# A decoder layer on one core: block rows spread by a VectorE transpose, decay rows loaded from DRAM, two groups of transposes moved to other slots

## The reference, cut to what matters

```
h = rms_norm(x)
all projections = h @ w_in                      # 2048 x 12304
branch A (8 heads x 128): causal softmax attention with ALiBi, times silu(gate)
branch B (8 heads x 128): short conv + silu on q, k, v; gated delta rule, per-head norm, times silu(gate)
x = x + (sigmoid(gA) * (A @ w_a) + sigmoid(gB) * (B @ w_b)) @ w_out ; rms_norm
```

## Time and profile before

| | |
|---|---|
| median of 3 runs | 800.74 us (800.04 to 801.30) |
| the profiled execution | 799.87 us |
| its span in the trace | 798.2 us |
| PE busy | 787.4 us (99%) |
| PE weight loads | 650.2 us (81%) |
| DVE busy | 519.4 us (65%) |
| ACT busy | 408.6 us (51%) |
| POOL busy | 103.3 us (13%) |
| loaded and stored | 142 MB, 178 GB/s |

### The profile page before, as it was taken

One profiled execution on the slowest core, in us unless ns is written; L12 is line 12 of the kernel. 1 busy time (PEld: TensorE's weight loads), 2 busy tenths in 40 slices (PEclk: granted clock), 3 DMA queues, 4 the chain that ended last, 5 costly groups with the idle time before them and its releaser, 6 DMA issues.

```text
span 798.2 us, 12578 instructions
## 1 busy us (share of the span) xinstructions
PE 787.4 (99%) x3712; PEld 650.2 (81%) x3712; DVE 519.4 (65%) x1030; ACT 408.6 (51%) x625; POOL 103.3 (13%) x174
## 2 busy tenths in 40 slices
PE   8999999999999999999999999999999999999996
PEld 7878888888888888888888888888888888888884
DVE  5687558646855785487558647855784556765563
ACT  5755545545554645455455455554545654444450
POOL 7020201110101012010201110101012000001120
PEclk9999999999999999999999999999999999999998
DMA  9946655575656555746655565656555666578652
GB/s 248 261 126 182 173 160 172 153 201 157 184 158 164 167 168 160 196 144 183 183 159 163 162 189 144 184 158 188 154 178 160 186 198 191 173 252 273 202 165 106
DMA packets 179225, 142.16 MB, mean 178 GB/s; under 512 B 10897, under 2 KB 144257, under 8 KB 179073
## 3 DMA queue, kind: packets, MB, share of 16 engines
q1 hardware_dynamic: 179056, 141.59, 61.2%
q10 hardware_dynamic: 144, 0.26, 0.1%
HBM read 139.72 MB, written 2.10 MB: 178 GB/s over the span
## 4 chain that ended last, share of the span: by engine, by line
PE 95%; DVE 2%; issue 1%; DMA 1%; ACT 0%; SPq 0%; POOLq 0%; POOL 0%; DVEq 0%; ACTq 0%
PE pj L542 28%; PE pj L540 28%; PE pj L541 28%; PE dn_ps L592 1%; DVE w_lo L1082 1%; PE pj L828 1%; PE pj L827 1%; PE pj L826 1%; PE dn_ps L621 1%; PE dn_ps L616 1%; DMA w_raw<-in_w_in_dram 1%; PE dn_ps L579 1%; PE dn_ps L605 0%; DVE conv L1202 0%; PE mo_ps L651 0%
## 5 line engine op out<-in xcount | busy, mean ns | idle before, releaser
L1082 DVE TENSOR_TENSOR w_lo<-w_raw,w_hi 128x1024 fp32r<-128x1024 f32 x251 | 309.5, 1236 | 163.6 <-ACT w_hi L842 162.4
L540 PE MATMUL pj<-w_hi,xt_hi 128*128 128x512 f32 x860 | 350.0, 407 | 0.3 <-DVE w_lo L1082 0.3
L542 PE MATMUL pj<-w_hi,xt_lo 128*128 128x512 f32 x860 | 337.4, 392 | 0.0
L541 PE MATMUL pj<-w_lo,xt_hi 128*128 128x512 f32 x860 | 335.5, 390 | 0.0
L842 ACT ACTIVATE w_hi<-w_raw 128x1024 fp32r<-128x1024 f32 x251 | 263.0, 1056 | 109.6 <-PE pj L542 98.0
L542 PEld LDWEIGHTS pj<-w_hi,xt_lo 128*128 128x128 f32 x860 | 161.4, 188 | 35.4
L540 PEld LDWEIGHTS pj<-w_hi,xt_hi 128*128 128x128 f32 x860 | 161.9, 188 | 31.1 <-ACT gate L991 1.1
L541 PEld LDWEIGHTS pj<-w_lo,xt_hi 128*128 128x128 f32 x860 | 162.1, 188 | 30.1
L936 ACT ACTIVATE ysb<-dn_ps 128x128 f32<-128x128 f32 x24 | 6.7, 278 | 69.8 <-PE dn_ps L616 69.8
L475 POOL TENSOR_TENSOR xo<-v,own 128x128 f32<-128x128 f32 x24 | 18.4, 766 | 185.5 <-DVE v L1279 102.0
L1261 DVE SCALAR_TENSOR_TENSOR xs<-lrep,xs 128x15 f32<-128x15 f32 (+14 forms) x240 | 35.0, 220 | 0.0
(11 more groups left out here) (292 smaller groups left out, 753.2 us busy)
## 6 DMA issues: line engine op xcount, KB each, us to landing
w_raw<-in_w_in_dram SPq DMA_DIRECT2D x384, 256.0 KB, 3.1
w_raw<-in_w_out_dram SPq DMA_DIRECT2D x64, 256.0 KB, 3.8
w_raw<-in_w_branch_a_dram SPq DMA_DIRECT2D x32, 256.0 KB, 3.3
w_raw<-in_w_branch_b_dram SPq DMA_DIRECT2D x32, 256.0 KB, 3.5
gate<-in_x_dram SPq DMA_DIRECT2D x8, 256.0 KB, 5.2
gate<-in_x_dram SPq DMA_DIRECT2D x4, 512.0 KB, 7.6
gate<-in_final_norm_gain_dram SPq DMA_DIRECT2D x1, 1024.0 KB, 9.3
out_dram<-gate SPq DMA_DIRECT2D x4, 256.0 KB, 3.5
```

Of the source, the lines that this page charges most:

```text
L540: pe.matmul(bank[:, t, :], hi[:, k, tok], w_hi[:, slot, cs], start=(k == 0), stop=False)
L541: pe.matmul(bank[:, t, :], hi[:, k, tok], w_lo[:, slot, cs], start=False, stop=False)
L542: mm = pe.matmul(bank[:, t, :], lo[:, k, tok], w_hi[:, slot, cs], start=False, stop=(k == kt_all - 1))
L1082: dve.tensor_tensor(w_lo[:, slot, :], w_raw[:, slot, :], w_hi[:, slot, :].bitcast(F32), ALU.subtract).then_inc(lo_ready, 1)
```

## The change

Four edits:

1. The spreading of `wc` no longer uses PE and ACT. The reduction now gives even and odd blocks apart (`wc` is 128x32), DVE transposes it in 32x32 blocks, each column repeated 16 times (`turned`, 128x512), and one DVE addition of the two halves, read with a stride, gives `lrep` (128x256). `blocks`, `spread` and slot 28 are gone.
2. The decay rows of heads 1 to 7 no longer come from PE. In head 0 the sixteen cumulated columns are turned once on PE, copied by DVE, stored by SP in DRAM (`cum_rows`), and from head 1 on SP loads two rows, repeated over 128 partitions, into `cum_row` (128x2x128) behind the loads of the head's unit 2. DVE reads them from SBUF.
3. The transposes of branch B's output move from slot 61 to slot 66 (slot 18 of the next head, ahead of the q, k, v transposes), and DVE's `yb_lo` to the slot after it.
4. Branch A's q and k transposes move from slot 34 to 36, behind the first doubling product, and the logits from 36 to 38.

```
-S_SPREAD = 28
-S_Y0, S_R1, S_Y1, S_O, S_YT = 51, 53, 55, 57, 61
+S_Y0, S_R1, S_Y1, S_O, S_YT = 51, 53, 55, 57, 66
-M_TURN, M_QK, M_EXP, M_PT, M_PV, M_YT = 34, 36, 40, 42, 44, 46
+M_NAT, M_TURN, M_QK, M_EXP, M_PT, M_PV, M_YT = 32, 36, 38, 40, 42, 44, 46
@@ SP
+                    if first and j == UNITS // 3 * 2:
+                        sp.wait_ge(cum_turned, 1)
+                        sp.dma_start(cum_rows.rearrange("t (h p) -> (t h) p", p=P), cumT[:, :]).then_inc(cum_stored, 16)
+                    if not first and j == 2:
+                        sp.wait_ge(cum_stored, 16)
+                        sp.dma_start(cum_row[:, :, :], cum_rows[:, bass.ds(head_col, P)].rearrange("(a t) n -> a t n", a=1).to_broadcast([P, T, P])
+                                     ).then_inc(cum_landed, 16)
@@ PE
-                if s == (S_DEC_FIRST if first else S_DEC):
+                if first and s == S_DEC_FIRST:
                     pe.wait_ge(hs_ready, h + 1)
-                    if not first:
-                        pe.wait_ge(ya_ready, T * h)
+                    pe.wait_ge(cum_cols_ready, T)
+                    pe.transpose(E[0:T * H, 2 * P:3 * P], cum_cols[:, :, :].rearrange("p t h -> p (t h)"), ident[:, :])
...
-                if s == S_SPREAD:
-                    pe.wait_ge(spread_ready, h + 1)
-                    pe.wait_ge(kk_ready, 3 * (h + 1))
-                    pe.matmul(A[:, 0:BS * BS], blocks[:, :], spread[:, :, :].rearrange("p j i -> p (j i)"),
-                              start=True, stop=True).then_inc(spread_done, 1)
...
-                    if n == 0:
-                        pe.wait_ge(lrep_ready, h + 1)
@@ ACT
-                if s == S_SPREAD:
-                    act.wait_ge(spread_done, h + 1)
-                    if not first:
-                        act.wait_ge(sub_step, 2 * (BS - 1) * h)
-                    act.activation(lrep[:, :, :].rearrange("p j i -> p (j i)"), A[:, 0:BS * BS], ACT.Copy).then_inc(lrep_ready, 1)
@@ DVE
+                dve.tensor_copy(cum_cols[:, 0, :], cum[:, 0, 0, :]).then_inc(cum_cols_ready, 1)
+                dve.tensor_copy(cum_cols[:, 1, :], C[:, 192:192 + H]).then_inc(cum_cols_ready, 1)
...
+                    if first:
+                        dve.tensor_copy(cumT[:, :], E[0:H * T, 2 * P:3 * P]).then_inc(cum_turned, 1)
...
-                    if not first:
-                        dve.wait_ge(spread_done, h)
-                    dve.tensor_reduce(wc[:, :], diag[:, :].rearrange("p (b i) -> p i b", i=BS), AX_X, ALU.add).then_inc(wc_ready, 1)
+                    dve.tensor_reduce(wc[:, :, :], diag[:, :].rearrange("p (b e i) -> p i e b", e=2, i=BS), AX_X, ALU.add
+                                      ).then_inc(wc_ready, 1)
                     dve.wait_ge(wc_ready, h + 1)
-                    dve.tensor_tensor(spread[:, :, :], wc[:, None, :].to_broadcast([P, BS, BS]),
-                                      delta[:, :, None].to_broadcast([P, BS, BS]), ALU.mult).then_inc(spread_ready, 1)
+                    dve.transpose(turned[:, :, :].rearrange("p i n -> p (i n)"),
+                                  wc[:, :, :, None].to_broadcast([P, BS, 2, BS])).then_inc(turned_ready, 1)
+                    dve.wait_ge(turned_ready, h + 1)
+                    if not first:
+                        dve.wait_ge(sub_step, 2 * (BS - 1) * h)
+                    dve.tensor_tensor(lrep[:, :, :], turned[:, :, 0:BS].rearrange("p i j -> p j i"),
+                                      turned[:, :, BS:2 * BS].rearrange("p i j -> p j i"), ALU.add).then_inc(lrep_ready, 1)
...
-                if s == S_YT:
+                if s == S_YT + 1:
                     dve.wait_ge(yb_hi_ready, h + 1)
```

More of the change, by code:

```diff
@@ L107, in build @@
         earlier = sb("earlier", [P, P])
-        blocks = sb("blocks", [P, P])
         blocks_neg = sb("blocks_neg", [P, P])
@@ L139, in build @@
         decay = sb("decay", [P, 5, P])
+        cum_row = sb("cum_row", [P, T, P])
+        cum_cols = sb("cum_cols", [P, T, H])
+        cumT = sb("cumT", [T * H, P])
+        cum_rows = nc.dram_tensor("cum_rows", (T, H * P), F32, kind="Internal").ap()
         vb = sb("vb", [P, T, P])
@@ L145, in build @@
         diag = sb("diag", [P, P])
-        wc = sb("wc", [P, BS])
-        spread = sb("spread", [P, BS, BS])
+        wc = sb("wc", [P, BS, 2])
+        turned = sb("turned", [P, BS, 2 * BS])
         lrep = sb("lrep", [P, BS, BS])
@@ L203, in build @@
         taps_ready, hs_ready, dec_done = sem("taps_ready"), sem("hs_ready"), sem("dec_done")
+        cum_cols_ready, cum_turned, cum_stored, cum_landed = sem("cum_cols_ready"), sem("cum_turned"), sem("cum_stored"), sem("cum_landed")
         dn_turned, conv_step, convs_ready, nat_done = (sem(n) for n in (
@@ L211, in build @@
         w_ready, v_ready, vT_done, vt_ready = sem("w_ready"), sem("v_ready"), sem("vT_done"), sem("vt_ready")
-        diag_ready, wc_ready, spread_ready, spread_done, lrep_ready = (sem(n) for n in (
-            "diag_ready", "wc_ready", "spread_ready", "spread_done", "lrep_ready"))
+        diag_ready, wc_ready, turned_ready, lrep_ready = (sem(n) for n in (
+            "diag_ready", "wc_ready", "turned_ready", "lrep_ready"))
         xs_set, sub_step, xc_ready = sem("xs_set"), sem("sub_step"), sem("xc_ready")
@@ L403, in _ @@
             pool.wait_ge(const_step, done)
-            pool.tensor_copy(blocks[:, :], own[:, 0, :]).then_inc(const_step, 1)
             pool.tensor_tensor(blocks_neg[:, :], ones[:, :], own[:, 0, :], ALU.subtract).then_inc(const_step, 1)
@@ L408, in _ @@
             pool.tensor_tensor(diag[:, 0:64], ident[:, 0:64], ident[:, 64:128], ALU.add).then_inc(const_step, 1)
-            done += 4
+            done += 3
             pool.wait_ge(const_step, done)
@@ L597, in dn_step @@
                         pe.transpose(C[:, t * P:(t + 1) * P], convs[:, (4 + t) * P:(5 + t) * P], ident[:, :])
-                    pe.wait_ge(dsub_ready, 5 * (h + 1))
+                    if first:
+                        pe.wait_ge(dsub_ready, 5)
+                        pe.wait_ge(cum_turned, 1)
+                    else:
+                        pe.wait_ge(ya_ready, T * h)
                     for t in range(T):
@@ L957, in mo_step @@
             def mo_step(s, h, first=False):
-                if s == M_TURN - 2:
+                if s == M_NAT:
                     if not first:
@@ L1174, in dn_step @@
                 if s == (S_DEC_FIRST if first else S_DEC):
-                    dve.wait_ge(dec_done, h + 1)
-                    if not first:
-                        dve.wait_ge(kk_ready, 3 * h)
-                    e1 = E[:, 2 * P - 1:P - 1:-1]
-                    e1_flip = E[:, P:2 * P]
-                    for block, t, e, mask in ((D00, 0, E[:, 0:P], later), (D11, 1, e1, later_flip),
+                    dve.wait_ge(hs_ready, h + 1)
+                    if first:
+                        dve.wait_ge(dec_done, 1)
+                    else:
+                        dve.wait_ge(cum_landed, 16 * h)
+                        dve.wait_ge(kk_ready, 3 * h)
+                    e = E[:, 0:2 * P] if first else cum_row[:, :, :].rearrange("p t n -> p (t n)")
+                    e0 = e[:, 0:P]
+                    e1 = e[:, 2 * P - 1:P - 1:-1]
+                    e1_flip = e[:, P:2 * P]
+                    for block, t, e, mask in ((D00, 0, e0, later), (D11, 1, e1, later_flip),
                                               (D11R, 1, e1_flip, earlier)):
@@ L1241, in dn_step @@
                     dve.wait_ge(diag_ready, h + 1)
[L1242 to L1247 removed]
+                    dve.tensor_reduce(wc[:, :, :], diag[:, :].rearrange("p (b e i) -> p i e b", e=2, i=BS), AX_X, ALU.add
+                                      ).then_inc(wc_ready, 1)
+                    dve.wait_ge(wc_ready, h + 1)
+                    dve.transpose(turned[:, :, :].rearrange("p i n -> p (i n)"),
+                                  wc[:, :, :, None].to_broadcast([P, BS, 2, BS])).then_inc(turned_ready, 1)
+                    dve.wait_ge(turned_ready, h + 1)
+                    if not first:
+                        dve.wait_ge(sub_step, 2 * (BS - 1) * h)
+                    dve.tensor_tensor(lrep[:, :, :], turned[:, :, 0:BS].rearrange("p i j -> p j i"),
+                                      turned[:, :, BS:2 * BS].rearrange("p i j -> p j i"), ALU.add).then_inc(lrep_ready, 1)
                     dve.wait_ge(q_squared, T * (h + 1))
```

1 line of the change is left out of this document (removed).

## The result

| | before | after |
|---|---|---|
| median | 800.74 us | 793.47 us (793.22 to 793.71, 5 runs) |
| the profiled execution | 799.87 us | 793.47 us |
| its span | 798.2 us | 791.8 us |

The ratio of the times is 0.991, with a 95% interval of 0.9897 to 0.9924. The kernel is 7.3 us faster on the medians, where the prediction said 4.8.

What follows compares the result with a forecast made beforehand. PE, busy 99% of the span, was taken as the bound. PE work and wait removed, 5.4 us, less 0.45 for head 0 and 0.2 of waiting, gave 4.8: from the 800.74 median to 795.9 us, range 794.6 to 799.0.

Steps and rivals of the forecast that it cites:

- the price of a visit: Small PE work between large matmuls: cost goes with columns alone, 0.43 us for the spread product, 0.22 for two decay transposes.
- fixed part: PE's cost for a visit as such: 15 moved visits by 0.01, 0.15 us at most, left out of the sum.
- spread visit gone: PE at slot 28: eight spread products removed, 0.43 us each, 3.4 us in all.
- The prediction's own sign of this error: Wrong if the visits' fixed part is real and merged PE visits give back more than 1 us.
- Head 0's cost: One more PE transpose and three small DVE copies in head 0: 0.45 us lost, ends 0 and 0.6.
- Slack: DVE's `xe` ahead of PE's weight load at slot 36: 0.69 us before, +0.06 after, no wait in the loop.
- wait in head 0: PE was expected to wait about 0.2 us in head 0, where the slack is smaller.
- the step: DVE's transpose, addition and `qn` ahead of slot 36: 1.45 us, ends 1.0 and 2.5.
- the second case: PE waits a little at slot 36 every head, 0.3 us each, 2.4 in all; 798.3 us; chance 0.24.
- the third: DVE bounds slot 36: step 2.5 us, PE waits about 1.0 us a head; 803.7 us; chance 0.06.
- the gain get lost elsewhere: Another wait, such as a late split of weights on DVE, takes the whole gain; 800.7 us; chance 0.07.
- More than the sum: Head 0 loses nothing and PE visits had a fixed part: 5.4 + 0.15, or 795.2 us; chance 0.03.

Runs made afterwards that it cites:

- the last one above: The changed kernel plus two unused tensors of 448 bytes, giving operands the low nine address bits of before; median 794.20 us, ratio to before 0.992.
- The spreading alone: The kernel before with only the spreading of `wc` moved to DVE; median 795.72 us, ratio 0.994.

## Why the prediction was wrong in its size

**The step that failed** is the price of a visit: "Price goes with columns, and nothing is left over for the visit as such", with a fixed part of 0.15 us at most in all, left out of the sum. The price was read to the second large matmul behind a visit, and for two visits only. Up to there it goes with columns nearly, not fully: two passes of 128 columns cost 0.223 us as the decay transposes and 0.242 as a doubling product before. The next ten matmuls are slower too, and that part I never looked at. Kernels with equal low addresses (before, and the last one above) give the account of a loop head without the address effect, by price and tail of each visit:

| a loop head | price | tail | together | predicted |
|---|---|---|---|---|
| spread visit gone | 0.433 | 0.040 | 0.473 | 0.43 |
| decay visit gone | 0.223 | 0.010 | 0.234 | 0.22 |
| q, k transposes merged | 0.018 | 0.062 | 0.080 | 0 |
| output transposes merged | 0.010 | 0.010 | 0.020 | 0 |
| old addresses: 74.41 to 73.60 | 0.68 | 0.12 | 0.81 | 0.65 |
| new addresses: 73.60 to 73.48 | 0.03 | 0.09 | 0.12 | - |

The fixed part takes 0.16 us a head beyond the prediction (some 1.2 us over the kernel) and the addresses 0.12 (some 0.9). Both terms were missing, the first named in the text and sized from a view that ends too early, the second not thought of. With them the sum is 4.8 + 1.2 + 0.9 = 6.9 us, against 7.3 measured. Head 0's cost and the waits (below) bring it to 7.0; the 0.3 that is left is less than the runs of one kernel spread (800.04 to 801.61 before). The prediction's own sign of this error, merged visits that give back more than 1 us, came only nearly: the two merges give 0.10 us a head, 0.8 in all, and the tails of the removed visits the rest.

**Head 0's cost** was taken as 0.45 us and measured 0.22: the Gram visit went from 1.95 to 2.06 us and the decay visit with its third transpose from 0.22 to 0.33. The choice inside the range of 0 to 0.6 was too dear by 0.23.

**The waits.** Slack 0.09 against 0.06, step 1.46 against 1.45, wait in head 0 of 0.25 against 0.2: the results of the account held, and no wait came in the loop. That the slack came out so near is in part luck, for two terms erred by 0.1 against each other. PE's load came 294.19 - 275.39 = 18.80 us behind the Gram product before and 290.96 - 273.13 = 17.83 after, 0.97 sooner where I had 0.87: the tails again. And DVE reached the step only 0.25 later (279.39 - 273.13 = 6.26, before 281.40 - 275.39 = 6.01), where I had 0.34 for `yb_lo`. Within the step the addition took 0.636 us where I had 0.55, the transpose 0.711 where I had 0.72. Head 1 waits 0.10 us, a term I did not have, since I took it for a head like the others. That the first substitution step waits for no other engine, as the section on the change has it, is not quite so: it still waits for POOL's small copy to `xs`, which is done 3.7 us ahead of it here (at 279.41, the step starts at 283.12).

The sum of the traces, from the starts of the Gram products: up to head 0's 51.61 before and 52.19 after, head 0 to head 1 74.97 and 73.84, then 74.41 and 73.61, five heads with 74.41 and 73.48, and from head 7's to the end 225.13 and 224.71. That is +0.58 - 1.13 - 0.80 - 4.65 - 0.42 = -6.4 us, the difference of the profiled executions. The start holds 0.31 us that is no part of the change: the twentieth large matmul starts at 13.49 us before and at 13.80 after, and anywhere from 13.44 to 14.51 in the fourteen traces. Without it the two traces differ by 6.7 us. The medians differ by 7.3 and the profiled executions by 6.4 because the profiled one before was 0.9 us faster than its kernel's median, while the one after was the median. Where those 0.9 us lie no trace shows; the start, which moves by as much between traces, is a guess.

**The rivals.** No head waits in the loop, so neither the second case (waiting 0.3 us) nor the third (DVE bound) came; nor did the gain get lost elsewhere. "More than the sum" came, which I gave 0.03 and a time of 795.2. Its ingredients were partly right: head 0 was cheap, though not free, and there is a fixed part, eight times as large as I had it; the addresses were in no case at all. The range's lower end rested on that factor: I had bounded the fixed part by the difference of two prices read from the same short view, and so both came without their tails.

**What the other steps gave.** The decay differences no longer wait; the rows' load lands long ahead of its use (issued at 79.2 us, read at 112.6 in head 1). From the changed kernel's DMA issues (size, median us to landing):

```profile
cum_row<-cum_rows SPq DMA_DIRECT2D x7, 128.0 KB, 3.4
...
cum_rows<-cumT SPq DMA_DIRECT2D x1, 8.0 KB, 2.3
```

**What stays open.** No run shows why a tail is 0.01 in one visit and 0.04 in another, or what in the matmul path reads the low part of an address. That tails depend on the visit's kind and on the addresses is shown; the mechanism is not. Nor is it known which operand's address it is. The spreading alone gives 0.57 a head, 0.09 more than its price and tail. Its trace shows where: in visits that the edit leaves alone (the tail of the q, k transposes is 0.022 in place of 0.047, that of `y` and `kk` 0.022 in place of 0.041, twice a head). It shifts the tensors behind `wc` by 64 bytes, so the addresses are the likely cause, but I ran no kernel of it with the old ones.

## What to carry to other kernels

Where one engine is the bound and small work stands between long runs of equal instructions, read the price of the small work up to the point where the intervals are back at their plain length, not to the next instruction or two: here most visits of 0.22 to 0.9 us had 0.01 to 0.07 us more behind that point, and merging two visits saved 0.08 us in one place and 0.02 in another without removing a column. When a predicted gain is a sum of small terms, compare also a whole period (here one head) with the sum of its known parts, since that shows what no single row shows. And a difference of 0.1% between two versions may come from where their tensors lie: an unused tensor of 64 bytes is a cheap control.

## What the runs showed of the hardware

- Ten large matmuls (128x512, fp32r) behind a visit of small float32 products take 2.28 to 2.34 us where they take 2.27 elsewhere; the granted clock was 1.00 in each head's window shown.
- The price of the small products and the tail change with the low part of the SBUF addresses of their operands: one head 74.41 us, and 74.35 with all tensors behind one shifted by 64 or by 1600 bytes, 74.40 by 1024; 73.48 and 73.60 in the changed kernel.
- DVE transposes 128x512 in float32 in 0.711 us, 128x128 in 0.312: per element little more than half. Beside POOL's products, which run from 279.36 in the second of these rows,

```profile
279.20 0.21 POOL L485 COPY xs<-delta 128x32 f32<-128x32 f32 x1
279.36 0.89 POOL L483 TENSOR_TENSOR mt<-w,levels 128x128 f32<-128x128 f32 x2
```

  the transpose at 279.39 takes 0.71 us. All eight transposes run beside these products, so no row shows one alone; that it wasn't held is not shown, but POOL's two products took 0.89 us here and 1.06 beside `spread` before, so the two got less into each other's way. The addition starts at 280.23, as those products end (280.25), and still takes 0.636 us where `yb_lo` of the same size takes 0.424. So the excess is not POOL's doing. Nor is it that both inputs lie in SBUF, as far as the split shows, which has that too and takes 1.23 us for four times the elements. That it is the reading with a step of 32 elements was argued and not tried; the Trainium skill (SBUF — State Buffer, section "Door 1: The DMA port swizzle") has a penalty for crossing 16-byte lines, and this row agrees in sign.
- A DVE delay ahead of a waiting PE product shows as 0.32 us in the product's row where the visit lost 0.58.
